# Low score products of layer 1 on half the array's rows, at the head of a step

## The reference

```python
q, k, v, g = jnp.split(h @ w_in, ...)            # q, k with rope
def block(i):                                    # 128 queries
    s_loc = einsum('bqhgd,bkhd->bhgqk', qs, ks) * scale   # key blocks i-1, i, i+1
    s_loc = jnp.where(valid, s_loc, NEG_INF)
    s_ctx = einsum('bqhgd,bkhd->bhgqk', qs, kc) * scale   # all 256 context keys
    p = softmax(concatenate([s_loc, s_ctx, sink]))
    return einsum(p[local], vs) + einsum(p[ctx], vc)
y = (o * silu(g)) @ w_o
# context queries: the same against the 256 context keys
```

## Time and profile before

| | |
|---|---|
| median of 3 runs | 1159.51 us (1159.49 to 1160.32) |
| profiled execution | 1159.5 us |
| its span, first to last instruction | 1157.7 us |
| TensorE busy | 1099.8 us, 95% |
| VectorE, ScalarE, GpSimd busy | 734.3, 649.0, 419.3 us |
| granted TensorE clock | 0.997 |

### The profile page before, as it was taken

The page is one execution under the profiler, slowest core; times in us unless marked ns, Lnnn a source line. Parts: engine busy times, 40 slices in busy tenths (PEclk is TensorE's granted clock), DMA queues, the critical chain, the costliest instruction groups (busy, mean ns, idle before and its releaser), DMA issues.

```text
span 1157.7 us, 20235 instructions
## 1 busy us (share of the span) xinstructions
PE 1099.8 (95%) x7430; PEld 900.7 (78%) x7430; DVE 734.3 (63%) x1590; ACT 649.0 (56%) x1355; POOL 419.3 (36%) x513
## 2 busy tenths in 40 slices
PE   5999999999998899999899999999999999999996
PEld 2678778877885689877688887898878777888785
DVE  7575766676568625363787787745767775527745
ACT  5604555555556526643677777846567753457733
POOL 2633012212120334675400002416654326456781
PEclk9999999999999999999999999999999999999998
DMA  9741424322114521130201101053212403213112
GB/s 373 253 163 46 176 107 162 133 108 101 46 29 173 204 81 37 40 109 35 57 14 34 65 10 47 1 166 87 73 46 78 151 19 128 91 56 121 44 37 73
DMA packets 34253, 109.33 MB, mean 94 GB/s; under 512 B 4516, under 2 KB 7076, under 8 KB 33772
## 3 DMA queue, kind: packets, MB, share of 16 engines
q1 hardware_dynamic: 34156, 108.05, 27.7%
HBM read 101.39 MB, written 2.11 MB: 89 GB/s over the span
## 4 chain that ended last, share of the span: by engine, by line
PE 75%; DVE 12%; ACT 5%; issue 3%; POOL 2%; DMA 2%; SPq 1%; DVEq 0%; POOLq 0%; ACTq 0%
PE PS L677 31%; PE PS L660 15%; PE PS L794 8%; PE PS L782 7%; PE PS L983 6%; PE PS L1051 3%; DMA AF<-wstream 2%; PE PS L712 2%; DVE AD L2372 1%; ACT AF L1272 1%; DVE AF L2069 1%; POOL AR L2553 1%; DVE AR L2273 1%; PE PS L884 1%; PE PS L693 1%
## 5 line engine op out<-in xcount | busy, mean ns | idle before, releaser
L2553 POOL TENSOR_TENSOR AR<-AF,AR 128x256 fp32r<-128x256 f32 x396 | 304.5, 802 | 585.2 <-ACT AR L1152 585.2
L677 PE MATMUL PS<-AR 128*128 128x512 f32 (+1 forms) x2208 | 450.5, 360 | 4.7 <-POOL AR L2553 1.4
L677 PEld LDWEIGHTS PS<-AR 128*128 128x128 f32 x2208 | 364.0, 189 | 72.6 <-issue 10.5
L660 PE MATMUL PS<-AR 128*128 128x256 f32 (+4 forms) x1284 | 244.9, 327 | 6.7 <-ACT AF L1272 1.7
L660 PEld LDWEIGHTS PS<-AR 128*128 128x128 f32 (+1 forms) x1284 | 179.8, 190 | 41.7 <-issue 20.6
L1281 ACT ACTIVATE AF<-PS 128x512 f32<-128x512 f32 (+3 forms) x192 | 124.6, 649 | 100.0 <-PE PS L782 96.0
L1272 ACT ACTIVATE AF<-PS,AF 128x512 f32<-128x512 f32 (+3 forms) x192 | 140.8, 733 | 27.2 <-DVE AF L2349 18.3
L782 PE MATMUL PS<-AF 128*128 128x128 f32 x864 | 127.4, 274 | 8.4 <-DVE AF L1990 5.9
L782 PEld LDWEIGHTS PS<-AF 128*128 128x128 f32 x864 | 100.1, 140 | 32.9 <-issue 15.5
L1152 ACT ACTIVATE AR<-AF 128x1024 fp32r<-128x1024 f32 x99 | 103.3, 1052 | 35.3 <-PE PS L983 27.9
L794 PE MATMUL PS<-AF 128*64 128x128 f32 x1728 | 115.3, 278 | 3.4 <-DVE AF L1997 2.5
(11 more groups left out here) (216 smaller groups left out, 1147.2 us busy)
## 6 DMA issues: line engine op xcount, KB each, us to landing
AF<-wstream SPq DMA_DIRECT2D x171, 512.0 KB, 5.0
AF<-x_in SPq DMA_DIRECT2D x2, 1024.0 KB, 8.5
AD<-rows SPq DMA_DIRECT2D x4, 512.0 KB, 5.9
out<-AF SPq DMA_DIRECT2D x16, 128.0 KB, 1.9
AF<-AF SPq DMA_DIRECT2D x28, 64.0 KB, 2.0
AF<-rpb_band SPq DMA_DIRECT2D x8, 224.0 KB, 5.2
BIAS<-rpb_band SPq DMA_DIRECT2D x8, 224.0 KB, 4.7
AF<-ctx_in SPq DMA_DIRECT2D x1, 1024.0 KB, 5.5
```

What stands on the lines that cost most here:

```text
L660: mm = pe.matmul(out, stationary, moving, start=i == 0, stop=i == len(products) - 1)
L677: mm = pe.matmul(out[:, 0:t1 - t0], a, b, start=k == 0 and i == 0, stop=k == nk - 1 and i == 2)
L2553: ins = pool.tensor_tensor(w[:, 1, at:at + 256], raw(c)[:, at:at + 256], w[:, 0, at:at + 256].bitcast(F32), ALU.subtract)
```

## The change

Three edits. The product with `KAL` is taken out of each segment; in its place every unit has a list `low`: the same segments in reversed order, with the 64 rows of the head's high part on both sides (`q[ROWS_OF[half]]`, `KAL[ROWS_OF[half]]`), so that low x low is no longer computed. `scores_low(m)` issues these for both units of a step, head beside head, at the step's beginning and opens the banks; the products of `scores` then add to them. It waits for both exponentials of step m-1. And in this layer the value products are no longer ahead of the second scores but at the step's end, behind the fillers. Layers 2 and 3 keep their order.

```diff
-                        segments = [(at, n, [(q, KA[:, tile, half, keys]), (q, KAL[:, tile, half, keys])])
-                                    for at, n, keys in places]
+                        segments = [(at, n, [(q, KA[:, tile, half, keys])]) for at, n, keys in places]
+                        low = [(at, n, q[ROWS_OF[half]], KAL[ROWS_OF[half], tile, half, keys]) for at, n, keys in places[::-1]]
...
-                    mm = sum_of(score_bank(n)[:, c0:c0 + width], products)
+                    mm = sum_of(score_bank(n)[:, c0:c0 + width], products, begun="low" in u)
...
+            def scores_low(m):
+
+                pe.wait_ge(exp_done, 2 * m)
+                for a, b in zip(units[2 * m]["low"], units[2 * m + 1]["low"]):
+                    for n, (c0, width, stationary, moving) in ((2 * m, a), (2 * m + 1, b)):
+                        pe.matmul(score_bank(n)[:, c0:c0 + width], stationary, moving, start=True, stop=False)
...
                         banks_read(m == m0, 0, 1)
+                        if "low" in units[2 * m]:
+                            banks_read(m == m0, 2, 3)
+                            scores_low(m)
                         scores(2 * m)
...
-                    ahead = values_first or m == m1
+                    ahead = values_first and "low" not in units[2 * m0] or m >= m1
                     if ahead and m0 <= m - behind - 1 < m1:
                         weigh_values(m - behind - 1)
...
+                    low = "low" in units[2 * m0]
+                    if low and (m < m1 or values_first):
+                        for name in fillers(m):
+                            make(name)
                     if not ahead and m0 <= m - behind - 1 < m1:
                         weigh_values(m - behind - 1)
-                    if m < m1 or values_first:
+                    if not low and (m < m1 or values_first):
                         for name in fillers(m):
                             make(name)
```

More of the change, by code:

```diff
@@ L541, in build @@
                             c0, c1, m0, places, blocks = S - C, S + wide, 0, [(S - C, C, both), (S, wide, own)], [4, 5] + near
-                        segments = [(at, n, [(q, KA[:, tile, half, keys]), (q, KAL[:, tile, half, keys])])
-                                    for at, n, keys in places]
+                        segments = [(at, n, [(q, KA[:, tile, half, keys])]) for at, n, keys in places]
+                        low = [(at, n, q[ROWS_OF[half]], KAL[ROWS_OF[half], tile, half, keys]) for at, n, keys in places[::-1]]
                         g0 = 64 * (2 * tile + half)
-                        unit(c0=c0, c1=c1, segments=segments, scale=SCALE_A, bias=MASK[:, m0:m0 + c1 - c0],
+                        unit(c0=c0, c1=c1, segments=segments, low=low, scale=SCALE_A, bias=MASK[:, m0:m0 + c1 - c0],
                              sink=col("sink", 2 * p + half), half=half,
@@ L592, in is_c, with is_b @@
             return n >= 2 * B_END
+        def is_b(n):
+            return 2 * A_END <= n < 2 * B_END
         def score_bank(n):
@@ L656, in chunk_ready, with sum_of @@
                 pe.wait_ge(lo_done, split_at[name] + 1)
-            def sum_of(out, products):
+            def sum_of(out, products, begun=False):
                 for i, (stationary, moving) in enumerate(products):
-                    mm = pe.matmul(out, stationary, moving, start=i == 0, stop=i == len(products) - 1)
+                    mm = pe.matmul(out, stationary, moving, start=i == 0 and not begun, stop=i == len(products) - 1)
                 return mm
```

## The result

The changed kernel takes 1195.47 us (median; 1193.54 to 1199.65) against 1159.88 of the kernel before beside it (1159.49 to 1160.32): 1.031 times as long (1.0294 to 1.0325). So it is slower, as forecast, but by 36 us instead of 11, and the time lies above the range. The profiled execution took 1194.4 us, its span 1192.6. Lines behind L542 have moved: L663 is a score product (L660 before), L680 a projection (L677), L715 a modulation row (L712), L784 a low product (new), L792 a transpose (L782), L804 a value product (L794), L1298 ScalarE's copy of transposes (L1281), L1289 the exponential (L1272), L2007 the end of `normalise` (L1990), L2014 `gate_output` (L1997), L1811 and L1984 the reads of bank 7 (L1794, L1967).

The account below looks back on a forecast made before the run. TensorE, busy 95% of the span, was taken as the bound. 1159.5 us - 10.3 (products) + 7.6 (changes of form) + 7.0 + 2.8 + 3.8 (filler waits) + 0.4 (other waits) = 1170.8 us, range 1158.5 to 1179.

Parts of the forecast that it names:

- What V covered: Value products moved behind the filler: filler comes 1.2 to 1.9 us sooner after first scores, adding waits of +7.0, +2.8, +3.8.
- Position 0: First query tile of a pair, after a modulation-row filler: filler waits 1.7 us for bank 7, four times, +7.0.
- (c): In a position-0 step the filler waits 1.7 us for bank 7's read; the value products' end releases gate_output.
- Position 5: Second context tile of a pair: filler waits 0.7 us for the previous filler's gate, four times, +2.8.
- Position 4: First context tile of a pair: filler waits 1.4 us behind a longer ScalarE and VectorE chain, 0.95 more, four times, +3.8.
- Products, -10.3: Layer 1's low products: two 64-row products take the time of one, saving 0.29, 0.24 or 0.12 us a step.
- changes, +7.6: Changes of the array's form in layer 1: three per step instead of two, one more at 0.17 us; +7.6 together.
- (a): Two heads' low products start within 0.01 us of each other; a pair takes 0.12 (256 columns) or 0.17 us (384).
- rival 2: The two row halves of the low products don't overlap, so the 10.3 us aren't saved: 1179 us; chance 0.12.
- Others, +0.4: Remaining layer 1 waits: low's wait for both exponentials and related waits -1.0, step 0 +0.4, steps 41 to 48 +1.0.
- (d): The modulation-row filler waits 0.7 us for the previous filler's gate; a projection filler waits 1.4 us for bank 7's read.
- Rivals 3 and 4: Third: array work alone decides, 1157.2 or 1153 us, chance 0.15; fourth: added waits up to 4.6 us, 1160, chance 0.11.

Follow-up runs that it names:

- e1: Changed kernel with the value products back between first transposes and second scores, half-row low products still at the step's head; 1170.33 us.
- e4: Changed kernel with the value products between the second scores and the second transposes, half-row low products kept; 1169.03 us.
- e9: Changed kernel with layer 1's gate_output moved behind the second normalisation of a step on VectorE; 1187.99 us.
- e10: e9 with the fillers also read ahead of VectorE's first row maximum; 1187.36 us.
- e3: Changed kernel with 128-row low products instead of 64-row ones, same order; 1190.94 us.
- e7: Changed kernel with first transposes and value products ahead of the scores, filler reads before the first row maximum, 128-row products inside the scores; 1173.65 us.
- e11: Kernel before with the filler reads ahead of VectorE's first row maximum in layer 1; 1165.02 us.
- e15: e1 with 128-row low products instead of 64-row ones; 1164.98 us.
- e8: Changed kernel with low products issued head by head instead of head beside head; 1195.48 us.
- e14: Changed kernel with low, then value products between second scores and second transposes, and filler reads before the first row maximum up to step 28; 1159.84 us.

## Why the prediction was right in sign and wrong in size

**The step that failed** is the list under "What V covered": I asked of V's move only what V had covered for the filler (bank 7), and never listed T1. Its wait was put at nothing without a reason; the list closes with "At V itself and at the bank of the outputs nothing waits", which is nearly so (one wait of 0.5 us), but beside the point. The code names it (`turn` waits for the copy) and so do the rows: ScalarE's copy takes 0.70 us for five tiles, and S1 after the change lasts 0.4. That much could have been worked out blind: the copy starts at T0's end, and S1's last product is issued 0.04 before that end, so nearly the whole 0.70 is left open. In step 8 T1 comes 0.93 us after S1's last start (153.59), where it needs 0.18. Added up from the starts in the two traces, T1 comes later than the array would allow (0.12 to 0.18 behind two or more score products, 0.22 behind a lone one, as in e1) by 33.9 us in the stage after, 30.1 of them behind the copy and 3.9 behind `normalise`, against 1.4 before; T0's lag fell from 4.2 to 0.2. Net **+28.5**, predicted none. The waits view shows 26.5 of the 33.9 (23.6 and 2.9), as a score product's span is modelled 0.16 us longer than its slot and so hides the head of each wait. e1 and e4 give 25 and 26 back.

**Filler waits, +13.6, was right in mechanism and too large.** Position 0: F comes 3.28 us after V's last start (139.06 to 142.35), predicted 3.3, and `gate_output` is released by V's end at 139.38, as written in (c). But T1 had already waited, so only 1.07 of the 1.7 are left. e9 and e10 confirm it part by part. Position 5: F comes 0.06 us later than a change of form alone (0.7 of wait predicted, swallowed by T1's own 0.69). Position 4: predicted 1.4, and F starts right behind T1; the waits of T1 in steps 3 and 4, 0.8 each, are longer than the chain's lag. Against before, the filler waits are +4.3, +0.3 and -1.7 instead of +7.0, +2.8 and +3.8: **10.7 too much**. What the sum took no account of: waits in a row on one engine don't add; the first one pays for the next.

**Products, -10.3, and changes, +7.6: right together.** (Some of the sum's products are off by 0.1 to 0.2: 8 x 1.30 is 10.4, 4 x 1.7 is 6.8, 48 x 0.02 is 1.0. It changes nothing.) A low piece costs 0.43 us (positions 0 and 3), 0.49 to 0.50 (1 and 2) and 0.31 (4 and 5), where 0.43, 0.48 to 0.49 and 0.31 to 0.32 follow from the prediction's terms. Two heads' products start 3 ns apart (152.029 and 152.032; 152.313 and 152.316), as (a) says. The split is another: behind its first pair the second comes after 0.22 to 0.28, not 0.12 or 0.17 (as the second product of full rows does behind V, too), and a change of form between T, V, low and S takes 0.20 from the last start of one piece to the first of the next. The Trainium skill, TensorE: Matmul & The Clock Gate, Part 3, says that matmuls in different row groups run concurrently: the trace agrees with those 3 ns, and rival 2 is out. Halves against full rows in the same place (e3) save 0.9 us over the stage, where the prediction's terms give 10.3 less 48 x 0.19 for the change between low and S0, 1.2. The Trainium skill, TensorEngine Tiling (Array Packing), Key Properties, on the drain at a change of mode, weighed against this change: the trace agrees, 0.20 us instead of 0.12, and it ate the gain.

**Not in the prediction: the clock,** +3.7 us in the fillers of the profiled execution (156.1 against e3's 152.4) and 0.7 in the value products (36.7 against 36.0 from first to last starts), 4.4 together. **Others, +0.4:** step 0's first filler starts 0.8 later (99.19 against 98.36); low's waits for both exponentials are 1.8 us, as S0's were before 1.7, as long as T1's waits stand ahead; e1 shows 7.5 without them.

**The ledger.** Of +34.3 us, 11.3 were predicted; +28.5 (T0 and T1), -10.7 (fillers) and +4.4 (clock) make 33.5 with them. Some 0.8 us I have not placed. By the signs that the prediction set: (e) holds (VectorE 740.5 us, ScalarE 648.3, count 7430); (a) holds in the starts and not in the 0.12 or 0.17 of a pair; (c) holds in what releases L2014 and not in the filler's 1.7 us; (b) gave 42.8 us for a pair of the first kind instead of 41.3, (d) is wrong at both fillers. Rivals 3 and 4 are out; the kernel is outside of all four, since none had T1.

**What stays open** is why the clock falls. Kernels with the low products in halves run at 0.986 to 0.995 more often; but e7, e11 and e15 have such stretches without any half, and e9 with halves has one in the stage. Waits of TensorE come before the three of the kernel after: 1.7 us before the one at 99.19, 0.4 and 0.8 before 228.90 (step 18), 0.8 and 0.5 before 423.45. But e3 has the same 1.7 us at the same place without a fall, and in the kernel after steps 6 and 24 have the same two waits as step 18 and no fall. What decides was not isolated.

## What to carry to other kernels

When a piece of work is moved, list for every piece that stays behind what it waits for, each bank that it writes over and each engine's read of it, not only the waits near the place where the moved piece lands; here that list would have shown the copy of 0.70 us in nearly every step. Then go through the waits of a step in order and let each one use up the slack of the next, instead of adding them. Products on half the rows pay only where their two changes of form cost less than the pairs save; here, with one end of low a change of form anyway, they saved 0.1 us in the best step and lost 0.07 in the context's, and where both ends were new changes they cost 4 us in all (e1 against e15).

## What the runs showed of the hardware that I had not expected

- Products of the two row halves pair up whatever order they are issued in (e8: starts 152.05, 152.06, 152.34, 152.34 with one head's products issued first). Whether they are reordered on the way or in the array wasn't tried.
- Behind a change of form the second product of a group comes late, with halves and with full rows alike: 0.22 us after the first of 256 columns, 0.28 after one of 384, where the later ones of full rows follow in 0.12 and 0.18. In the kernel after it is the second pair (152.029, 152.313), in e3 the second full-row product (150.151, 150.436, then 150.611), in the kernel before the second of S1 behind V (156.092, 156.313, then 156.431). No row of 64-row pairs was longer than two, so what a pair costs in a long row isn't shown.
- Five transposes take 0.44 us to the fifth's start, 0.11 each; the next piece follows after 0.03 if it is a score product and after 0.20 if it is V. The 0.09 per change in the prediction was the difference of such figures and too low for a change with nothing under it.
- The granted clock fell to its lower level for 3.4 us at a time (three times in the stage of the kernel after, each at a cost of half its length, some 1.7 us), behind waits of TensorE of no more than 1.7 us, and not behind others as long. e14's runs, at granted clocks from 0.990 to 0.998, spread over 7 us (1156.05 to 1163.25).
